# Two transformer blocks on one core: the second expert stage split by rows, both front stages written in another order, the modulation vector made on TensorE

## The reference, cut to what matters

```python
# second block
mod = silu(c) @ w_ada + b_ada                      # 1024 -> 6*1024
shift1, scale1, gate1, shift2, scale2, gate2 = split(mod, 6)
h = rms_norm(x, g_norm1) * (1 + scale1) + shift1
proj = h @ w_in          # na_q na_k na_v q_lat kv_lat k_rot gate_na gate_mla
...
merged = sigmoid(gate_na) * (y_na @ w_proj_na) + sigmoid(gate_mla) * (y_mla @ w_proj_mla)
x = x + gate1 * (merged @ w_out)
h2 = rms_norm(x, g_norm2) * (1 + scale2) + shift2
scores = sigmoid(h2 @ w_router)                    # 64 experts in groups, 8 per token
...
hidden_e = silu(h2 @ w_exp_gate[e]) * (h2 @ w_exp_up[e]) * gates[:, e]
routed = sum_e hidden_e @ w_exp_down[e]            # shared = the same with w_sh_*, every token
x = x + gate2 * (routed + shared)
```

## Time and profile before

| | |
|---|---|
| median of 3 runs | 1619.62 us (1618.14 to 1623.03) |
| the profiled execution | 1610.28 us, of which the traced span 1608.3 |
| granted TensorE clock, mean | 0.856 of full |
| PE busy | 1250.0 us, 78% of the span, 4145 matmuls |
| DVE, ACT, POOL busy | 492.4, 245.3, 291.6 us |
| DMA | 380.47 MB, mean 237 GB/s |
| second expert stage, first to last gate/up product | 958.5 to 1550.0 us |

### The profile page before, as it was taken

The page is one execution under the profiler, slowest core; times in us unless marked ns, Lnnn a source line. Parts: engine busy times, 40 slices in busy tenths (PEclk is TensorE's granted clock), DMA queues, the critical chain, the costliest instruction groups (busy, mean ns, idle before and its releaser), DMA issues.

```text
span 1608.3 us, 12711 instructions
## 1 busy us (share of the span) xinstructions
PE 1250.0 (78%) x4145; PEld 637.8 (40%) x4145; DVE 492.4 (31%) x987; ACT 245.3 (15%) x513; POOL 291.6 (18%) x249
## 2 busy tenths in 40 slices
PE   5979587686656659988888839889889888798870
PEld 3444544452212224447564424434434444344430
DVE  4989522321001032013713342222212222222216
ACT  2011312201000110015321101111111111111110
POOL 7999970000000000000000010000000000000004
PEclk9989588769878889996969859999989999899995
DMA  9895340089999994420403057898888888888847
GB/s 298 289 360 183 92 132 0 26 337 417 422 422 421 421 362 125 157 85 1 157 5 106 1 196 265 262 319 278 276 306 276 299 298 274 303 278 298 310 170 235
DMA packets 178148, 380.47 MB, mean 237 GB/s; under 512 B 20172, under 2 KB 111528, under 8 KB 165768
## 3 DMA queue, kind: packets, MB, share of 16 engines
q1 hardware_dynamic: 156776, 304.42, 52.9%
q0 software_dynamic: 15152, 53.14, 9.9%
q10 hardware_dynamic: 6192, 22.55, 3.4%
HBM read 354.39 MB, written 26.64 MB: 237 GB/s over the span
## 4 chain that ended last, share of the span: by engine, by line
PE 45%; DMA 31%; DVE 15%; SPq 3%; ACT 3%; issue 2%; POOL 0%; DVEq 0%; ACTq 0%; POOLq 0%
DMA wring<-in_w_exp_up 16%; PE bank L699 15%; PE bank L879 12%; DMA wring<-in_w_pack 10%; PE bank L865 5%; PE bank L710 2%; PE bank L739 2%; PE bank L835 2%; DVE wring L1740 2%; PE bank L856 1%; DMA PR<-y_dram,y_rows 1%; ACT PR L1121 1%; PE bank L728 1%; DMA PR<-in_mem 1%; DVE tmp L1321 1%
## 5 line engine op out<-in xcount | busy, mean ns | idle before, releaser
L879 PE MATMUL bank<-wring,qT 128*128 128x512 f32 x672 | 337.4, 661 | 77.3 <-DMA wring<-in_w_exp_up 72.0
L699 PE MATMUL bank<-wring,hT 128*128 128x512 f32 (+3 forms) x608 | 251.3, 578 | 15.4 <-DMA wring<-in_w_in 6.8
L879 PEld LDWEIGHTS bank<-wring,qT 128*128 128x128 f32 x672 | 139.3, 213 | 248.0 <-issue 248.0
L699 PEld LDWEIGHTS bank<-wring,hT 128*128 128x128 f32 x608 | 116.5, 203 | 146.9 <-issue 135.8
L622 POOL COPY token_now<-token_list 128x1 uint32 (+1 forms) x43 | 8.4, 195 | 896.6 <-PE bank L856 503.0
L1697 DVE TENSOR_TENSOR PT<-bank,PT 128x256 f32<-128x256 f32 x42 | 17.8, 425 | 467.5 <-ACT PT L1158 467.5
L865 PE MATMUL bank<-wring,PT 128*128 128x512 f32 x344 | 156.5, 598 | 2.6 <-ACT PT L1161 2.6
L818 PE MATMUL bank<-wring,qT 128*32 128x512 f32 x512 | 76.0, 749 | 51.4 <-DMA wring<-in_w_pack 49.9
L1687 DVE TENSOR_SCALAR qT<-bank,gs,modc 128x128 f32<-128x128 f32 x344 | 113.6, 403 | 5.0 <-PE bank L856 3.5
L606 POOL TENSOR_SCALAR wring<-wring,silc 128x1024 f32<-128x1024 f32 x32 | 93.6, 2926 | 12.6 <-DMA gateB<-in_b_ada 8.1
L865 PEld LDWEIGHTS bank<-wring,PT 128*128 128x128 f32 x344 | 62.6, 192 | 65.7 <-issue 62.8
(11 more groups left out here) (348 smaller groups left out, 1220.6 us busy)
## 6 DMA issues: line engine op xcount, KB each, us to landing
wring<-in_w_pack SPq DMA_DIRECT2D x96, 1024.0 KB, 20.1
wring<-in_w_exp_gate SPq DMA_DIRECT2D x42, 1024.0 KB, 9.3
wring<-in_w_exp_up SPq DMA_DIRECT2D x42, 1024.0 KB, 11.7
wring<-in_w_exp_down SPq DMA_DIRECT2D x42, 1024.0 KB, 7.4
wring<-in_w_in SPq DMA_DIRECT2D x12, 2048.0 KB, 14.6
y_dram<-PR ACTq DMA_DIRECT2D x43, 512.0 KB, 6.7
wring<-in_w_ada POOLq DMA_DIRECT2D x32, 512.0 KB, 4.3
wring<-in_w_out SPq DMA_DIRECT2D x4, 2048.0 KB, 10.4
```

Of the source, the lines that this page charges most:

```text
L699: mm = nc.tensor.matmul(b[:, 0:n], lhs(k, t), w[:, k, c0:c0 + n], start=(k == 0), stop=(k == nk - 1))
L879: mm = nc.tensor.matmul(bank[0:rows_n, 2, :], xT[:, s, k, 0:rows_n], ring_gu(s)[:, k, :], start=(k == 0), stop=(k == KD - 1))
```

## The change

The change has four parts.

A. **The second expert stage is split by rows.** Experts with more than 32 rows stay items of 128 rows (`items()`), those with 1 to 32 rows go four at a time through the same code as in the first expert stage (`quads(2, pairs)`), behind the items. By the counts above that is 22 items in 11 pairs and 5 quads. All expert weights come from `w2_pack`, packed by the host so that each partition's part is contiguous: gate and up together as one 2 MB load (16 KB per partition), down as 1 MB. The first of the three weight groups of the first quad is loaded while the items run, the second waits for the last item's gate/up, the third for its down. The rows of large experts are still stored to `y_dram` and gathered by token, 16 gathers, which are now issued behind the row gathers of quads 1 and 2 (`result_gathers`), and DVE adds them between the steps of the first quads. A token's choice that went to a small expert has no row in `y_dram`; its index is 0 and its weight 0. So that whatever is gathered is a finite number, all 8320 rows of `y_dram` are first written with a row of `gateB`, by nine stores on SP (8 x 4 MB and one of 512 KB, L573), and ACT waits for them before the first result is stored. The small experts' sum lies in PSUM banks 4 to 7 and is added last.

B. **Front 2 in another order.** `y.0`, `y.1`, `y.3`, `y.2` first; `y.4` to `y.7` (the gates) stand between the steps of the two attentions, and ACT takes their sigmoid as it empties the bank. The mla normalisation is beside `y.4` and `y.5`. `pmla`, the merge, `wout2`, the norm and `route2` go by halves of 128 tokens. ACT and DVE share the emptying of the turned x. The routing on DVE follows `route2` at once and the shared expert is put into its gaps.

C. **The modulation vector on TensorE.** 27 steps (three groups of eight row blocks of `w_ada` and a bias row), each four products with a 32-column stationary silu(c) on four column groups side by side (L967, L970), in PSUM bank 7. POOL only issues the loads, 27 of up to 1 MB, into four buffers, the first after the choice of keys. POOL's and DVE's arithmetic and PE's L994 and L1000 are gone.

D. **Front 1 in another order.** The index scores are made between the chunks of z and the choice of keys begins earlier on DVE, `z.3`, `z.4`, `z.5` and the memory chunks follow beside it. All front weights are packed by the host (16 KB contiguous per partition for a 2 MB block).

```diff
 def plan_jobs():
-    two = [(f"y.{c}", "w_in_2", a, n, 8) for c, (a, n) in enumerate(Y_CHUNKS)]
-    two += [("uq", "w_uq_2", 0, 768, 2), ("ukv", "w_ukv_2", 0, 1024, 1),
-            ("pna", "w_proj_na_2", 0, 1024, 4), ("pmla", "w_proj_mla_2", 0, 1024, 4),
+    two = y_jobs(0, 1, 3, 2)
+    two += [("uq", "w_uq_2", 0, 768, 2), ("ukv", "w_ukv_2", 0, 1024, 1)]
+    two += y_jobs(4, 5) + [("pna", "w_proj_na_2", 0, 1024, 4)]
+    two += y_jobs(6, 7) + [("pmla", "w_proj_mla_2", 0, 1024, 4)]
...
 # SP: a front weight block
-                sp.dma_start(slot_of(job), A[src][0][:, c0:c0 + n].rearrange("(k p) n -> p k n", p=P))\
-                    .then_inc(E(f"weights_loaded{j % SLOTS}"), 16)
+                sp.dma_start(slot_of(job).rearrange("p k n -> p (k n)"), A[f"pack_{job}"]).then_inc(E(f"weights_loaded{j % SLOTS}"), 16)
...
 # SP: the weights of an item
-                        for c0, w in ((0, gate), (FF, up)):
-                            sp.dma_start(gu[:, :, c0:c0 + FF], w[bass.ds(e, 1)].rearrange("o (k p) n -> p (o k) n", p=P))\
-                                .then_inc(E(f"moe{n}_gate_up_loaded{s}"), 16)
+                        sp.dma_start(item_gate_up(s).rearrange("p k n -> p (k n)"), A["w2_pack"][bass.ds(e, 1), :, 0:4096].rearrange("o p n -> p (o n)"))\
+                            .then_inc(E(f"moe2_gate_up_loaded{s}"), 16)
...
 # SP: the quads' weights, three groups of four 1 MB blocks
-                        elif g == 1:
-                            sp.wait_ge(E("bank_filled"), last_use("mod"))
+                        elif n == 1 and g == 1:
+                            sp.wait_ge(E("ada_steps_made"), ADA_GROUPS * ADA_STEPS)
+                        elif n == 2 and g == 0:
+                            continue
+                        elif n == 2:
+                            sp.wait_ge(E(("moe2_gate_up_made", "moe2_down_made")[g - 1]), pairs * 2 + 1)
...
 # SP: behind each of the last nine weight blocks of front 2
+                if n >= len(jobs[1]) - 9:
+                    a = n - (len(jobs[1]) - 9)
+                    blocks = min(8, WHOLE + 1 - 8 * a)
+                    sp.dma_start(y_dram[8 * a * P:(8 * a + blocks) * P].rearrange("(b p) d -> p b d", p=P),
+                                 gateB[:, 1:2, :].broadcast_to([P, blocks, D])).then_inc(E("y_filled"), 16)
...
 # PE: one step of the modulation vector
+                for q in range(ada_made[0], ada_made[0] + count):
+                    g, k = q // ADA_STEPS, q % ADA_STEPS
...
+                    pe.wait_ge(E(f"ada_loaded{q % ADA_BUFFERS}"), 16 * (q // ADA_BUFFERS + 1))
+                    for j in range(4):
+                        if k < KD:
+                            mm = nc.tensor.matmul(bank[lane[j], 7, :], silc[:, k:k + 1].broadcast_to([P, SLAB]), w[:, 512 * j:512 * (j + 1)],
+                                                  start=(k == 0), stop=False)
...
 # POOL: the second expert stage's quads
+                    for t in range(2):
+                        pool.wait_ge(E("moe2_quad_rows_turned"), t + 1)
+                        gather(t + 1, "moe2_quad_tokens", t + 1)
+                        result_gathers(t)
```

More of the change, by code:

```diff
@@ L159, in plan_groups @@
-    two = [(f"xT4.{i}", V) for i in range(4)]
-    two += [(f"y.{c}.{t}", A) for c in range(8) for t in range(2)]
+    one += scores("dsa", (2, 4))
+    one += [("kv.0.0", A), ("kv.0.1", A)] + probs("dsa", 0, 2) + [("kv.1.0", A), ("dsa.o.0", V)] + probs("dsa", 1, 4)
+    one += [("kv.1.1", A), ("dsa.o.1", V), ("kmT.0", A), ("kmT.1", A), ("dsa.yT.0", A), ("dsa.yT.1", A)]
+    one += columns("wout", V)
+    one += [("xT2.0", V), ("xT2.1", V), ("wq.0", A), ("xT2.2", V), ("xT2.3", V), ("wq.1", A)]
@@ new lines, in plan_groups @@
+    one += [("qmT.0", A), ("qmT.1", A), ("modT.0", A)]
+    one += scores("mem", (2, 2))
+    for t in range(2):
+        one += probs("mem", t, 2) + [(f"mem.o.{t}", V)]
+    one += [("modT.1", A), ("mem.yT.0", A), ("mem.yT.1", A), ("gate.0", A), ("gate.1", A)]
+    one += columns("wo", V)
+    for t in range(2):
+        one += [(f"xT3.{2 * t}", V), (f"xT3.{2 * t + 1}", V), (f"route1.{t}", V)]
+    one += [("rank1", V), ("modT.2", A), ("start1", V), ("gate.2", A), ("items1", V), ("gate.3", A), ("tokens1", V)]
@@ new lines, in plan_groups @@
+    two += scores("mla", (4, 4))
+    two += [("y.6.0", A), ("y.6.1", A)] + probs("mla", 0, 4) + [("y.7.0", A), ("mla.o.0", V)] + probs("mla", 1, 4)
+    two += [("y.7.1", A), ("mla.o.1", V), ("mla.yT.0", A), ("mla.yT.1", A)]
+    two += columns("pmla", V)
+    for t in range(2):
+        two += [(f"mgT.{2 * t}", A), (f"mgT.{2 * t + 1}", A), (f"wout2.0.{t}", V), (f"wout2.1.{t}", V)]
+    for t in range(2):
+        two += [(f"xT5.{2 * t}", A), (f"xT5.{2 * t + 1}", V), (f"route2.{t}", V)]
+    two += [("shgu.0", V), ("rank2", V), ("start2", V), ("items2", V), ("shgu.1", V), ("tokens2", V), ("shT.0", A), ("shT.1", A)]
@@ L1897, in _ @@
             quad_starts()
[L1898 to L1900 removed]
+            quads_opened(1)
+            quads(1, col("ffn_norm"), None)
+            for t in range(2):
+                for half in range(2):
+                    o = x[:, t, half * 512:(half + 1) * 512]
+                    link(V.tensor_tensor(o, bank[:, 4 + 2 * t + half, :], o, ALU.add))
+                signal("x_added")
+            copied(dve, "modT.2")
             for m, g in ((0, "g_norm1_2"), (1, "g_norm2_2")):
```

1704 lines of the change are left out of this document (932 added, 772 removed).

## The result

The changed kernel takes 1323.25 us (median of 4 runs, 1318.55 to 1326.04) against 1618.88 of the kernel before (4 runs, 1616.99 to 1623.03). The ratio is 0.8168 with an interval of 0.8139 to 0.8197: 296 us less. The forecast was 1355, so the gain was 12% larger than the 264 us forecast. The profiled execution took 1322.58 us, its span 1320.7.

What follows compares the result with a forecast made beforehand. DMA bound the first expert stage, PE and its waits front 2, late weight loads the second stage. 1608.3 - 23 - 48 - (591.7 - 264) + (192 - 58.1) = 1343.5; with 2.0 and 9.3, 1355; range 1305 to 1415.

Steps and rivals of the forecast that it cites:

- Front 2, projection to `wout2`: Second front's 273 us: `y.4` to `y.7` fill half of 59 us of gaps, 29 off, bounds 10 and 45.
- the next step: Behind `wout2` to the first item, 82 us: `route2` halves and earlier routing take 16 off, bounds 5 to 25.
- Front 1: Up to first issue of expert weights: 37 earlier at `wout`, modulation gives back 14; net -23, 327.3 to 304.
- All three terms: Modulation's 27 steps in front 1: 25 us on PE, 18 of them hidden in waits, 7 of waiting for loads.
- Items: Second expert stage: 22 items at 12.0 us with contiguous loads, 264 us, bounds 254 and 310.
- the room of 9.8 us: In an item: a weight landing up to 9.8 us after its issue is hidden; 4.19 MB take about that.
- Rival (a): Items keep 14.1 us because stores, gathers and weights share the engines: 46 more, 1401; chance 0.13.
- Quads of the second stage: From last gate/up to the end: 70.2 MB at 415 GB/s, 192 us in all, bounds 172 and 225.
- Rival (b): The fronts give only a third of the 71 us: 47 more, 1402; chance 0.17.
- Rival (c): Second-stage quads: result gathers and DVE's adds hold up the next quad's rows, 10 us lost at the changeover: 1385; chance 0.12.
- Rival (d): Stores over `y_dram` cost 6.7 us a block, 436 us, and eat the whole gain: 1620; chance 0.02.
- Rival (e): Second expert stage's split fails, all 42 items stay whole and only load faster: 1460; chance 0.01.

Runs made afterwards that it cites:

- The pair with and without fillers: Changed kernel with `y.4` to `y.7` ahead of the attentions and seven PSUM banks: 1352.46 us without, 1344.71 us with unread products in three waits.
- the order: SP issues the next gate/up load ahead of the wait for the down buffer: 1297.46 us on the changed kernel, 1521.5 us alone on the kernel before.

## Why the prediction was right, and where its sizes were off

The parts of the sum in their order, in us:

| | forecast | measured |
|---|---|---|
| first issue of expert weights | 304 | 294.5 |
| from it to the last landing of the first stage | 255 | 254.4 |
| from there to the last quad's sum | 8.5 | 8.5 |
| last quad's sum to the projection | 9.1 | 9.0 |
| projection to the end of `wout2` | 244 | 219.0 |
| end of `wout2` to the first item | 66.4 | 61.7 |
| items, 22 | 264 | 279.3 |
| from there to the end | 192 | 194.2 |
| span | 1343.5 | 1320.7 |
| around it and up to the median | 11.3 | 2.6 |

The total was met better than its terms, and that is partly luck. The fronts came out 40 us better than forecast, one more than the bounds together allowed (39), and the items 15 worse. Without the items' miss the time would have been 1308, just above the range's lower end of 1305.

- *Front 2, projection to `wout2`: mis-sized, 29 us forecast (bounds 10 and 45) and 54 gained.* The step took half of 59 us of gaps and no clock. But those gaps were counted from 600 to 950 us, and the stretch ends at 876: it had only 25.8 us of idle time in it, less than the 29 taken. The rest lay behind `wout2`, from where the next step took another 16. 22 of the 25.8 went, and the clock gave 32 more. So the 29 are not the half of anything in the trace: too much idle time and no clock made up for each other in part. The text even named the granted 0.87 and 0.80 and took them as a reason against the gain (a filled gap takes longer), while here it is the gap that keeps the clock low. The pair with and without fillers shows the direction.
- *Front 1: a gain in one step and a loss in another.* `wout` began at 152.3 and not at 168, again 20 us of clock that no step had. From `wout` to the first expert weights it then took 142.2 us where it was 122.3, 20 more and not 14; against no steps, in the reordered front, the modulation cost about 31 (25 to 32). All three terms were too kind: the steps were busy 33.6 us and not 25, waited 9.2 for loads and not 7, and filled some 10.5 us of waits (the 21 of them) and not 18. The waits that they were to fill were those of the kernel before (29.8 us in this stretch); 20.2 were left in the reordered front.
- *Items: the mechanism half right, 12.0 forecast and 12.7 measured.* That packing pulls the landing in was right: alone it gave 14.1 to 12.6. But the step compared the landing with the room of 9.8 us and never asked why the issue came 1.8 us into the item. SP's wait for the down buffer stood ahead of it, and that was worth more than the size of the pieces: alone in the kernel before 14.1 to 11.9. In the packed version the order brings 12.7 to 11.6; the items with the order but without the packing, in the kernel before, take 11.9, so the packing has 0.3 left to give. Rival (a), sharing as the cause, is refuted: the items run at 11.6 with the same transfers beside them.
- *Quads of the second stage: right.* DMA moved 412 GB/s from 1130 to 1300. The first two periods, with the result gathers beside them, were 39.5 and 42.3 us, the last two 31.2 and 31.1. Then come 8.5 us of PE, from the last down products to the last sum, and 8.8 of DVE (12 operations of 0.69). The last down products waited for ACT and not for a load. The Trainium skill, "DMA: Bandwidth & Descriptors", section "Where 436 GB/s comes from", has the HBM side bind at about 358 GB/s per core; this stretch, too, moved 54 GB/s more with the one core at work, and the measurement decides.
- *Rival (b)*: refuted, the fronts gave 111 us up to the first item (33 of it up to the first expert weights) and not a third of 71. *Rival (c)* is answered above by the gathers moved last. *Rival (d)*: its price of 6.7 us a block is latency; eight stores of 4 MB landed in a median of 19.3 us each, 2.4 a block, beside other loads. *Rival (e)*: 22 items and 5 quads ran.
- The last line, 8.7 us: the profiled execution of before lay 9.3 below its median, that of the changed kernel 0.7. Adding the offset of one kernel to another was worse here than adding nothing.

## What to carry to other kernels

Count a removed wait of TensorE twice: once for the wait, once for the products behind it that had run at half the clock. To size it, compare the busy time of the same number of products at both clocks in the table by stretches. Before a late transfer is blamed on its size, look at what its issue waited for: an engine that issues two kinds of loads, each behind its own wait, issues them in the order of its program, and the load that is free first must stand first. And when idle time is counted for a step, count it within that step's own stretch and as it will be behind the other edits: here 59 us of gaps reached 74 us past the end of the stretch, which held 26, and the modulation's steps were to hide in waits of which the reordering had already taken a third.

## What the runs showed of the hardware

- With gate and up loaded in 1 KB pieces DMA moved 337 GB/s, gathers and stores included, busy 0.96 of the time; packed ones 345 (the need of the items, not a limit) and 412 to 422 in the quad stages.
- A wait of PE can cost more than twice its length: behind a wait of 2.70 us (with one of 1.32 shortly ahead) 32 instructions took 7.09 us for 3.68 and the 16 behind them 3.43 for 1.92. In the changed kernel's items a wait of 2.54 us left the next 16 products at 7.11 us, one of 2.67 was followed by 8.53:

```profile
1090.49 8.53 PE L926 MATMUL bank<-wring,qT 128*128 128x512 f32 x16 [2.67 <-DMA wring<-in_w_pack]
```

- Useless products in the waits made a chain of real ones shorter by 7.7 us of 90.7, in one profiled execution of each.
- Stores of 34 MB of a broadcast row in 4 MB pieces made no product wait at a DMA share of 0.66, and twice as many cost 32 to 36 us.
